# Squared ReLU of the MLP's up projection: one fused VectorE instruction replaced by Relu and Square on ScalarE

## What is computed

```python
def sq_relu_mlp(h, w1, w2):
    return jnp.square(jax.nn.relu(h @ w1)) @ w2
...
x = x + g2 * sq_relu_mlp(modulate(rms_norm(x, norm_mlp_g[i]), sh2, sc2), mlp_w1[i], mlp_w2[i])
```

## Time and profile before

| what | value |
|---|---|
| median of 3 runs | 2640.75 us (2637.38 to 2641.97) |
| the profiled execution | 2644.23 us |
| its span, first to last instruction | 2642.4 us |
| TensorE matmuls busy | 2471.6 us (94% of the span) |
| VectorE busy | 1955.2 us (74%) |
| ScalarE busy | 1167.6 us (44%) |
| DMA, mean | 231 GB/s |
| mean granted TensorE clock | 0.964 of full speed |

### The profile page before, as it was taken

How to read it: one execution, slowest core, us unless ns; L and a number is a source line. 1 busy time by engine, 2 the same in 40 slices (tenths; PEclk the granted TensorE clock), 3 DMA queues, 4 the chain that set the end, 5 groups by cost and what they waited for, 6 DMA issues and landing times.

```text
span 2642.4 us, 40626 instructions
## 1 busy us (share of the span) xinstructions
PE 2471.6 (94%) x13316; PEld 2077.0 (79%) x13316; DVE 1955.2 (74%) x2322; ACT 1167.6 (44%) x1595; POOL 0.2 (0%) x4
## 2 busy tenths in 40 slices
PE   6879989798999999999989899899899999999998
PEld 2248867587888888888878778787788888888887
DVE  6767777687987878878878888888765565565665
ACT  2334256435344444444454325234544444444444
POOL 0000000000000000000000000000000000000000
PEclk9989998898999999999989999999899999999998
DMA  8857865576988888888777658576665565665653
GB/s 306 319 183 247 277 194 171 168 269 234 351 299 279 281 279 280 269 283 280 263 241 243 211 195 278 173 247 213 201 190 187 187 190 186 187 190 185 189 189 121
DMA packets 441193, 610.10 MB, mean 231 GB/s; under 512 B 18875, under 2 KB 383644, under 8 KB 439068
## 3 DMA queue, kind: packets, MB, share of 16 engines
q1 hardware_dynamic: 439676, 599.98, 68.4%
q10 hardware_dynamic: 1440, 9.18, 1.0%
HBM read 596.50 MB, written 10.49 MB: 230 GB/s over the span
## 4 chain that ended last, share of the span: by engine, by line
PE 71%; DVE 13%; issue 6%; ACT 6%; DMA 3%; SPq 0%; DVEq 0%; ACTq 0%
PE ps L359 42%; PE ps L368 22%; DVE acc L456 2%; DVE w_lo L444 2%; PE ps L1100 2%; ACT w_hi L440 2%; DMA raw<-in_mlp_w 1%; ACT hm L875 1%; DVE sm L1751 1%; DMA raw<-in_attn_w_out 1%; PE ps L1136 1%; PE ps L1117 1%; DVE u L646 1%; PE ps L1326 1%; ACT probs L1465 1%
## 5 line engine op out<-in xcount | busy, mean ns | idle before, releaser
L444 DVE TENSOR_TENSOR w_lo<-raw,w_hi 128x1024 fp32r<-128x1024 f32 x720 | 877.3, 1224 | 495.5 <-ACT w_hi L440 491.7
L440 ACT ACTIVATE w_hi<-raw 128x1024 fp32r<-128x1024 f32 x720 | 758.9, 1059 | 1030.5 <-PE ps L368 813.6
L359 PE MATMUL ps<-lat,w_hi 128*128 128x512 f32 x3136 | 816.2, 400 | 31.0 <-DVE lat L864 18.3
L359 PEld LDWEIGHTS ps<-lat,w_hi 128*128 128x128 f32 x3136 | 575.9, 192 | 140.1 <-issue 24.5
L359 PE MATMUL ps<-alt,w_hi 128*128 128x512 f32 x2624 | 674.4, 396 | 11.2 <-DVE alt L1738 5.9
L359 PEld LDWEIGHTS ps<-alt,w_hi 128*128 128x128 f32 x2624 | 476.3, 190 | 97.9 <-issue 6.7
L368 PEld LDWEIGHTS ps<-lat,w_lo 128*128 128x128 f32 x3136 | 435.3, 192 | 31.4 <-DVE w_lo L444 0.4
L368 PE MATMUL ps<-lat,w_lo 128*128 128x256 f32 x3136 | 447.6, 284 | 0.0
L456 DVE SCALAR_TENSOR_TENSOR acc<-slab,silu,acc 128x1024 f32<-128x1024 f32 x300 | 380.2, 1280 | 8.9 <-DMA slab<-in_mod_w 6.8
L368 PEld LDWEIGHTS ps<-alt,w_lo 128*128 128x128 f32 x2624 | 363.7, 192 | 26.4 <-DVE w_lo L444 0.6
L368 PE MATMUL ps<-alt,w_lo 128*128 128x256 f32 x2624 | 374.4, 283 | 0.2 <-DVE w_lo L444 0.2
(11 more groups left out here) (191 smaller groups left out, 1512.4 us busy)
## 6 DMA issues: line engine op xcount, KB each, us to landing
raw<-in_mlp_w SPq DMA_DIRECT2D x512, 512.0 KB, 3.7
slab<-in_mod_w SPq DMA_DIRECT2D x352, 512.0 KB, 5.9
raw<-in_hy_w_in SPq DMA_DIRECT2D x96, 512.0 KB, 6.6
raw<-in_attn_w_in SPq DMA_DIRECT2D x48, 512.0 KB, 4.6
raw<-in_mod_w SPq DMA_DIRECT2D x32, 512.0 KB, 6.7
raw<-in_attn_w_out SPq DMA_DIRECT2D x32, 512.0 KB, 4.9
raw<-in_hy_w_out SPq DMA_DIRECT2D x32, 512.0 KB, 7.0
spec_dram<-spec ACTq DMA_DIRECT2D x8, 1024.0 KB, 6.9
```

What stands on the lines that cost most here:

```text
L359: e.matmul(ps[:, bank, :], w_hi[:, n % RING, kk, fb * P:(fb + 1) * P], t[:, kb, :], start=(kb == 0), stop=False)
L440: e.activation(w_hi[:, n % RING], raw[:, n % RING], ACT.Copy).then_inc(hi_ready, 1)
L444: e.tensor_tensor(w_lo[:, n % RING], raw[:, n % RING], w_hi[:, n % RING].bitcast(F32), ALU.subtract).then_inc(split_ready, 1)
```

## The change

Nothing but the class `Hidden` is touched. VectorE's fused instruction goes. ScalarE's tail now waits for `psum_free` of its half (VectorE's sum) instead of `squared`, makes Relu and then Square in place in `sum_sb`, each counted in `squared`, waits for each by that semaphore, and then makes the same Copy into `alt` as before. VectorE's tail is unchanged and waits for the Copy.

```diff
--- before.py
+++ after.py
@@ -596,12 +596,14 @@
             def dve_head(self, e, T, g):
                 e.wait_ge(lo_copied, 2 * T + g + 1)
                 e.tensor_tensor(sum_sb[:, g], self.bank(g, 0), lo_sum[:, g], ALU.add).then_inc(psum_free, 1)
+
+            def act_tail(self, e, T, g):
                 e.wait_ge(psum_free, 2 * T + g + 1)
-                e.scalar_tensor_tensor(sum_sb[:, g], sum_sb[:, g], 0.0, sum_sb[:, g],
-                                       ALU.max, ALU.mult).then_inc(squared, 1)
-
-            def act_tail(self, e, T, g):
-                e.wait_ge(squared, self.n + 2 * self.i + g + 1)
+                before = 2 * (self.n + 2 * self.i + g)
+                e.activation(sum_sb[:, g], sum_sb[:, g], ACT.Relu).then_inc(squared, 1)
+                e.wait_ge(squared, before + 1)
+                e.activation(sum_sb[:, g], sum_sb[:, g], ACT.Square).then_inc(squared, 1)
+                e.wait_ge(squared, before + 2)
                 e.activation(alt[:, ds(4 * self.i + 2 * g, 2), 0:TOK], sum_sb[:, g], ACT.Copy).then_inc(hidden_hi, 1)
 
             def dve_tail(self, e, T, g):
```

## The result

Over 12 runs of each the changed kernel has a median of 2646.77 us (2643.83 to 2653.34), the kernel before 2641.85 us (2637.38 to 2645.88). The ratio is 1.002 with a 95% interval of 1.0011 to 1.0029: slower by 4.9 us, 2.9 to 7.7 by the interval. The forecast was 2640.7 us and no change. The time lies inside the stated range, but no change was forecast and there is one, to the slower side.

What follows compares the result with a forecast made beforehand. TensorE was taken to bound 56 of 64 places; waits held it back in layer 0's first up quarter. Three periods, turn and clock summed as 3 x (-0.5) + 1.0 + 0.4 = -0.1 us, giving 2640.7 us, range 2636 to 2647.

Steps and rivals of the forecast that it cites:

- The split of the kernel: MLP stages: 56 of 64 places under a full TensorE cost nothing; 8 in layer 0's first up quarter matter.
- The durations: ScalarE's added passes: Relu and Square taken at 0.63 us each, 128 passes making 81 us of busy time.
- the +1.0 taken: Turn from up to down in the first quarter: L610 starts at 740.6 instead of 739.60, TensorE waiting for it.
- Between -0.7 and +1.0 I take -0.5, nearest to the full queue of rows 6: First up quarter, each of three periods: 0.5 us shorter, because a full DMA queue begun earlier delivers by volume.
- less than about 6.0 us: Condition for the -0.7 per period: the last raw unit lands within this time of its issue, rather than 7.
- The stretched loop: Rival, chance 0.22: in the first quarter the last raw unit keeps its 7 us; up to +4.8 us, 2645.5.
- The relief: First up quarter: without L600, VectorE's w_lo of unit 0 comes 0.7 us earlier, and the queue's filling with it.
- The clock term: Turn: TensorE's wait growing to about 3 us costs 0 to 0.8 more at the lower clock; 0.4 taken.
- It decides from a wait of about 1.95 us: TensorE in the first quarter: a wait of about this length decides whether its clock falls to the lower level.
- a falling clock in the periods: Rival, chance 0.08: the +1.0 lands in TensorE's wait for L598, its clock falling each period; +9.9 us, 2650.6.
- VectorE's relief: Rival, chance 0.05: the loop loses both L600, 1.4 us a period, and the turn too; -7.3 us, 2633.5.
- table loads: Rival, chance 0.02: Relu and Square share no table, every tail paying two loads of 1283 ns; +25, 2666 us.

Runs made afterwards that it cites:

- all_but_first: Changed readout only in the 56 halves outside layer 0's first up quarter, the kernel before in that quarter; 2642.72 us, ratio 1.0004.
- raw_first: Changed kernel with SP issuing each slab pair one unit later in the first up quarter; 2645.23 us, ratio 1.0009.
- relief_only: Kernel before without VectorE's fused instruction, ScalarE keeping only its Copy, so the MLP is linear; 2638.55 us, ratio 0.9989.
- link_only: Kernel before with one more ScalarE Relu pass ahead of each Copy, VectorE's fused instruction kept; 2646.94 us, ratio 1.0023.
- late_tail: Changed kernel; in first-quarter up tiles ScalarE's half 0 tail stands behind its half 1 head, VectorE's low parts behind two slab steps; ratio 0.9999.
- late_tail_vector: Kernel before with ScalarE's half 0 tail and VectorE's low parts moved later in first-quarter up tiles; 2642.72 us, ratio 1.0001.
- raw_first_vector: Kernel before with SP issuing each slab pair one unit later in the first up quarter; 2643.16 us, ratio 1.0002.
- before_again: The kernel before profiled once more, nothing changed; periods 72.44 us, turn 12.43 us, rest 624.01 us.
- scalar_late_all: Changed kernel with later tails in first-quarter up tiles and VectorE's two reductions behind the first turn's last low part; 2641.62 us, ratio 0.9995.
- changed_again: The changed kernel run once more, nothing else changed; 2646.92 us, ratio 1.0018.
- first_only: Changed readout only in the 8 halves of layer 0's first up quarter, the kernel before in the other 56; 2646.9 us, ratio 1.0019.

## Why the prediction was wrong

*The split of the kernel* held. The 56 places under a full TensorE cost nothing (all_but_first), and the 8 others carry the whole result.

*The durations* held: 612 and 632 ns for 630, no table load. The first pass starts 0.04 us behind L598 instead of 0.10, but two gaps were larger than assumed: 0.14 us between Square and Copy in the loop, and 0.25 us between the Copy and L612. The likely reason for the second is two register operations of VectorE's queue, 99 and 40 ns, which the trace has ahead of L612 at 48 of its 64 places (the DVEq lines above), those in loops. In the period shown they stand at 682.68 and 682.82, behind the Copy's end at 682.65; before, at 688.15 and 688.29, they ran under VectorE's `w_lo`. In the turn, where the indices are constants, there are none and the gap is 0.03. No run tried it. So the slab pair moved by +1.17 us, not +1.0. In the turn the link is 2.70 us from L598 to L612 against 2.47, and the turn came to +0.85 for the +1.0 taken.

**The step that failed** is "Between -0.7 and +1.0 I take -0.5, nearest to the full queue of rows 6". Measured is +1.3 us a period, 4.0 over three: the term had the wrong sign, and its upper bound was too low as well. The step assumed that a queue which is full now stays fed when three of its entries are issued over a microsecond later. It does not. From the issue of unit 4's load (the last of the group of five, so 0.38 us before that group's end) to that of the slab pair it is 690.48 - 682.06 = 8.4 us before and 692.17 - 681.84 = 10.3 us after, and the thin spots of 271 and 308 GB/s go with it. What is issued in between, with unit 4's load, is three loads and four slabs of 512 KB each; at the 379 GB/s of the earlier trace rows they last 9.7 us, an estimate from these rows: longer than 8.4 and shorter than 10.3. SP's rows, first before, then after:

```profile
...
671.77 10.67 SPq L315 DMA_DIRECT2D raw<-in_mlp_w  x5
...
690.48 1.50 SPq L307 DMA_DIRECT2D slab<-in_mod_w  x2
...
```

```profile
...
672.32 9.90 SPq L315 DMA_DIRECT2D raw<-in_mlp_w  x5
...
692.17 1.50 SPq L307 DMA_DIRECT2D slab<-in_mod_w  x2
...
```

The load itself took about what it took before, 7.3 us from issue to use (693.92 to 701.22, before 692.24 to 699.25), so the condition "less than about 6.0 us" failed. The stretched loop was named as a rival at 0.22 with up to +4.8 us, 2645.5; that is the mechanism that held, and its sum of 3 x 1.0 + 1.0 + 0.8 comes close for partly compensating reasons: 3 x 1.3 + 0.85 and a clock term between 0 and 1.6. That the time lies inside the stated range comes from this rival, which the range was drawn to hold, and not from the forecast's sum. The prediction also expected this rival to be hidden within 0.2%; with 12 runs of each kernel the interval is 4.8 us wide and excludes zero. That the last raw unit alone carries the loss is not shown, since raw_first does not decide it.

*The relief* was overrated from the same cause. The prediction let an earlier start of the queue's filling, 0.7 us, come back as time. Shortening VectorE's part by 1.4 us a period gave 0.5 (relief_only), without the longer link.

*The clock term* was 0.4 for a longer wait. Between the two profiles of before and after it was nothing: the eight matmuls took 2.70 us against 2.95, and `rest` is 625.57 in both. What counts is whether the clock falls at all, see below: behind 2.8 us it fell each time, behind 1.95 not each time, so the prediction's "It decides from a wait of about 1.95 us" does not hold either.

*Its rivals:* in the changed kernel a falling clock in the periods did not come; the waits for `w_hi` grew instead (0.87, 1.65 and 0.33 us ahead of the three last units), which was the argument against it. VectorE's relief did not win, and nothing suggests table loads.

## What to carry to other kernels

Where an engine's in-order queue holds both a readout chain and the work that frees load buffers, cost a longer hop to another engine and the work taken off this one separately: here a hop that put the slab steps off by 1.3 us cost 1.6 us a period (link_only), and 1.4 us less of work gave 0.5 (relief_only). A DMA queue that shows as full is not a reserve: count what is outstanding when the late entry is issued. Before moving work between engines, try moving its place in the queue: here the place was worth some 5 us (the changed kernel at +4.9, late_tail at -0.1) and the engine nothing that could be measured (late_tail against late_tail_vector).

## What had not been expected of the hardware

TensorE's clock behind one and the same wait of 1.95 us differs between executions of the same code. It fell in three profiles of five (before, all_but_first, raw_first_vector) and stayed in two. In the kernel before it fell to 0.50, the 1.2 GHz level, and the eight matmuls took 2.95 us. In before_again it stayed at the full 2.4 GHz:

```profile
...
735.34 2.06 PE L359 MATMUL ps<-alt,w_hi 128*128 128x512 f32 x8 [1.95 <-DVE alt L610]
...
```

```profile
...
737.00:738.50 1.50, 1.50 (x12) 1.40 (x11) 1.50 (x2) 0.43 (x1) 0.00 (x0) 1.00 1.11 377
...
```

`rest` is 624.0 us in the profiles where it stayed (before_again, late_tail_vector, and with shorter waits relief_only and scalar_late_all) and 625.6 where it fell: a fall costs 1.6 us once (in link_only it lasted from 740.9 to 747.8 us, twice as long as elsewhere, and `rest` is 626.85). Behind the 2.79 us of the changed kernel it fell in each profile that has that wait; in the changed kernel itself:

```profile
...
745.00:746.50 1.50, 1.50 (x6) 1.21 (x5) 1.50 (x2) 0.00 (x0) 0.00 (x0) 0.50 1.02 380
...
```

Shorter waits within the periods can do it too. In link_only it fell at 700.0 us behind a wait of 1.73 us, in raw_first behind 1.78:

```profile
...
708.20 2.51 PE L364 MATMUL ps<-lat,w_hi 128*128 128x512 f32 x8 [1.78 <-DVE sum_sb L603]
...
710.75:711.75 1.00, 1.00 (x6) 1.00 (x6) 0.97 (x2) 1.00 (x2) 0.00 (x0) 0.50 0.79 228
...
```

Behind 1.76 us in changed_again (677.90) and behind 1.77 in the same raw_first (682.50) it stayed. The length of the wait alone does not decide it; what else does, no run here shows.

The second finding is the spread of the total. The start of this stage differs by up to 8.7 us between executions in untouched code (627.3 in link_only, 636.0 in first_only), more than the effect, so one span of each kernel would have shown nothing.
